# Moving the fourth pair's attention logits ahead of the output projection, with a fourth masked-logit buffer

## The reference, cut to what matters

```python
def block(args):                        # one block of 128 query rows, 8 heads
    ...
    _, sel = lax.top_k(iscore, topk)    # 256 keys chosen per row
    logits = jnp.einsum('bthc,btkc->bthk', ql_b, kv_sel)
    logits = jnp.where(valid[:, :, None, :], logits, -jnp.inf)
    probs = jax.nn.softmax(logits, axis=-1)
    return jnp.einsum('bthk,btkc->bthc', probs, kv_sel)
...
y_dsa = jnp.einsum('bshc,hcd->bshd', o_lat, w_uv[i]).reshape(B, S, DSA_WIDTH)
mix = jnp.concatenate([y_ret, y_dsa], axis=-1) @ w_out[i]
x = x + rms_norm(mix, post_mix_g[i])
f = rms_norm(x, pre_ffn_g[i])
```

## Time and profile before

| | value |
|---|---|
| three executions | 1429.82, 1430.89, 1433.61 us |
| span of the profiled execution | 1428.3 us |
| PE, DVE, ACT, POOL busy | 96%, 71%, 42%, 23% of the span |
| granted TensorE clock, mean | 0.995 |
| attention stage, 456 to 657 us | 201 us, PE busy 181.4 us |

### The profile page before, as it was taken

The page is one execution under the profiler, slowest core; times in us unless marked ns, Lnnn a source line. Parts: engine busy times, 40 slices in busy tenths (PEclk is TensorE's granted clock), DMA queues, the critical chain, the costliest instruction groups (busy, mean ns, idle before and its releaser), DMA issues.

```text
span 1428.3 us, 19391 instructions
## 1 busy us (share of the span) xinstructions
PE 1376.4 (96%) x7142; PEld 1125.8 (79%) x7142; DVE 1013.1 (71%) x1592; ACT 605.1 (42%) x1229; POOL 329.0 (23%) x383
## 2 busy tenths in 40 slices
PE   7999999999989889998999999999999999999998
PEld 7887888887777567777778888888887888888886
DVE  5748789998999546765877777777776765565633
ACT  6434552315823776574522222222222656453221
POOL 4545457711541475652000000000000000000000
PEclk9999999999999999999999999999999999999999
DMA  6322223225323021133234555444458866662211
GB/s 215 82 56 71 79 84 116 94 92 192 111 101 143 31 74 61 45 91 107 55 131 165 177 177 177 161 148 153 156 193 289 316 239 223 237 213 75 67 53 45
DMA packets 137150, 189.02 MB, mean 132 GB/s; under 512 B 12768, under 2 KB 75616, under 8 KB 137056
## 3 DMA queue, kind: packets, MB, share of 16 engines
q1 hardware_dynamic: 120224, 152.17, 32.5%
q10 hardware_dynamic: 16832, 35.61, 6.5%
HBM read 130.08 MB, written 57.67 MB: 131 GB/s over the span
## 4 chain that ended last, share of the span: by engine, by line
PE 79%; DVE 7%; issue 4%; ACT 4%; POOL 3%; DMA 1%; DVEq 1%; SPq 0%; ACTq 0%; POOLq 0%
PE ps L728 23%; PE ps L729 23%; PE ps L730 23%; PE ps L930 2%; PE ps L922 2%; PE ps L941 1%; PE ps L769 1%; POOL mxs L2721 1%; DMA raw<-in_w_in 1%; DVE sc L1915 1%; ACT lm L1444 1%; DVEq L1931 1%; PE ps L857 1%; PE ps L892 1%; PE ps L855 1%
## 5 line engine op out<-in xcount | busy, mean ns | idle before, releaser
L2593 POOL TENSOR_TENSOR smf<-smf,sml 128x1 f32<-128x1 f32 x16 | 9.1, 579 | 739.3 <-DVE smf L2474 625.2
L728 PE MATMUL ps<-bh,ah 128*128 128x512 f32 x308 | 120.1, 390 | 2.4 <-DVE u2b L2315 2.4
L730 PE MATMUL ps<-bh,al 128*128 128x512 f32 x308 | 119.9, 389 | 0.0
L729 PE MATMUL ps<-bl,ah 128*128 128x512 f32 x308 | 119.8, 389 | 0.0
L728 PE MATMUL ps<-wbh,xth 128*128 128x512 f32 (+1 forms) x320 | 118.9, 371 | 0.0
L729 PE MATMUL ps<-wbl,xth 128*128 128x512 f32 (+1 forms) x320 | 117.7, 368 | 0.0
L730 PE MATMUL ps<-wbh,xtl 128*128 128x512 f32 (+1 forms) x320 | 117.7, 368 | 0.0
L2421 DVE TENSOR_TENSOR al<-ra,ah 128x512 fp32r<-128x512 f32 x77 | 53.1, 690 | 70.7 <-ACT ah L1671 70.3
L728 PE MATMUL ps<-th,ssh 128*128 128x512 f32 x240 | 93.6, 390 | 1.8 <-DVE u2b L2291 1.2
L730 PE MATMUL ps<-th,ssl 128*128 128x512 f32 x240 | 93.4, 389 | 0.0
L729 PE MATMUL ps<-tl,ssh 128*128 128x512 f32 x240 | 93.4, 389 | 0.0
(11 more groups left out here) (375 smaller groups left out, 3871.1 us busy)
## 6 DMA issues: line engine op xcount, KB each, us to landing
raw<-in_w_in SPq DMA_DIRECT2D x49, 256.0 KB, 3.0
wt<-in_w_ffn_down SPq DMA_DIRECT2D x44, 256.0 KB, 7.2
down_sums<-wt ACTq DMA_DIRECT2D x44, 256.0 KB, 5.0
ra<-hidden_sums SPq DMA_DIRECT2D x44, 256.0 KB, 2.9
rb<-down_sums SPq DMA_DIRECT2D x44, 256.0 KB, 3.5
raws<-in_w_ffn_gate SPq DMA_DIRECT2D x21, 512.0 KB, 3.9
raws<-in_w_ffn_up SPq DMA_DIRECT2D x21, 512.0 KB, 5.3
ret_rows<-stg SPq DMA_DIRECT2D x32, 320.0 KB, 3.4
```

What stands on the lines that cost most here:

```text
L728: pe.matmul(o, ah, wh, start=start, stop=False, skip_group_check=resumes)
L729: pe.matmul(o, ah, wl, start=False, stop=False, skip_group_check=resumes)
L730: return pe.matmul(o, al, wh, start=False, stop=stop, skip_group_check=resumes)
```

## The change

The pair logits of step t+2 are issued in step t, behind the first part of the probability products and in front of the output projection, at the seven places. DVE masks head t+2 right behind head t+1, in step t+1, ahead of the search pieces and of the probability copy of that step. ACT takes the exponential of head t+1 in step t+1, in front of `read_mix`, instead of in step t+2 behind `mix_square`. A fourth LM tile is added (4 KB per partition at offset 200.5), and LM is used modulo 4, so that `mask_logits(t)` waits for the transposes of head t-4 instead of t-3. Since the new tile overlaps WL[1], `second_gate_lo` waits for the last transposes of LM. Nothing is computed that was not computed before, and no DMA is moved.

```diff
-    LM = [sb(f"lm{i}", [P, S], a) for i, a in enumerate((112, 116, 164))]
+    LM = [sb(f"lm{i}", [P, S], a) for i, a in enumerate((112, 116, 164, 200.5))]
...
+    def before_projection(t):
+
+        return at_block(t, OUT_LAG) is not None and t + 2 < STEPS
...
         for t in range(STEPS + TAIL):
-            if t < STEPS and t % 2 == 0:
+            if t < STEPS and t % 2 == 0 and not before_projection(t - 2):
                 pair_logits(t // 2)
...
+            if before_projection(t):
+                pair_logits(t // 2 + 1)
             if at_block(t, OUT_LAG) is not None:
                 out_projection(at_block(t, OUT_LAG), 0)
...
-            if 1 <= t <= STEPS:
+            if 1 <= t <= STEPS and not before_projection(t - 2):
                 exponent(t - 1)
+            if before_projection(t - 1):
+                exponent(t)
             if at_block(t, OUT_LAG + 1) not in (None, RT - 1):
                 read_mix(at_block(t, OUT_LAG + 1))
...
-            if t >= 3:
-                dve.wait_ge(s["t_tp"], tp_at[("tr", t - 3)] + 1)
+            if t >= len(LM):
+                dve.wait_ge(s["t_tp"], tp_at[("tr", t - len(LM))] + 1)
...
         def second_gate_lo():
             dve.wait_ge(s["a_gh"], 2)
+            dve.wait_ge(s["t_tp"], tp_at[("tr", STEPS - 1)] + 1)
...
-            if t < STEPS:
+            if t < STEPS and not before_projection(t - 2):
                 mask_logits(t)
+            if before_projection(t - 1):
+                mask_logits(t + 1)
```

More of the change, by code:

```diff
@@ L929, in prob_transposes @@
             for j in range(b + 1):
-                m = pe.transpose(pair(2)[:, j * P:(j + 1) * P], LM[t % 3][:, j * P:(j + 1) * P], ID)
+                m = pe.transpose(pair(2)[:, j * P:(j + 1) * P], LM[t % len(LM)][:, j * P:(j + 1) * P], ID)
             m.then_inc(s["t_tp"], 1)
@@ L1443, in exponent @@
             c = (b % 2) * H + h
-            sc.activation(LM[t % 3][:, 0:keys], LM[t % 3][:, 0:keys], ACT.Exp, scale=-1.0,
+            sc.activation(LM[t % len(LM)][:, 0:keys], LM[t % len(LM)][:, 0:keys], ACT.Exp, scale=-1.0,
                           bias=cols["nmax"][:, t % 4:t % 4 + 1], accum_out=cols["sum"][:, c:c + 1])\
@@ L2109, in mask_logits @@
             dve.wait_ge(s["t_lg"], t // 2 + 1)
-            if t >= 3:
-                dve.wait_ge(s["t_tp"], tp_at[("tr", t - 3)] + 1)
-            v.tensor_tensor_reduce(LM[t % 3][:, 0:keys], pair(t % 2, keys), mask, -1.0, 3.0e38, ALU.add, ALU.min,
+            if t >= len(LM):
+                dve.wait_ge(s["t_tp"], tp_at[("tr", t - len(LM))] + 1)
+            v.tensor_tensor_reduce(LM[t % len(LM)][:, 0:keys], pair(t % 2, keys), mask, -1.0, 3.0e38, ALU.add, ALU.min,
                                    cols["nmax"][:, t % 4:t % 4 + 1]).then_inc(s["v_lm"], 1)
```

## The result

The changed kernel took 1438.63 us (median of 4 runs, 1438.36 to 1439.59), the kernel before 1430.94 (4 runs on the same chip, 1429.82 to 1433.61): 1.0054 of before, 95% interval 1.0041 to 1.0067. The forecast was 1438.0 us.

What follows compares the result with a forecast made beforehand. PE, busy 96% of the span, was taken to bound the kernel, with waits at X3 for ACT's chain. 1428.3 + 6.1 (later X3) + 1.1 (DVE beside POOL) = 1435.5, with 2.6 for the median about 1438 us; range 1431.5 to 1442.

Steps and rivals of the forecast that it cites:

- The trade on PE and ACT: Seven places: moved logits and mask waits delay projections 10.8 us in all; exponentials leaving ACT's chain save 5.7 at most.
- the delay minus the exponential: Places 0 to 3, ACT's chain: X3 comes later by 1.04, 0.34, 0.68 and 0.55 us.
- X3's wait at places 0 to 3 smaller in PE idle time: Sign expected in the profile after: PE idles less at X3 there, though X3 comes later in time; no size given.
- Rival A: Seven places: logits cost 7.6, exponentials return 5.7, so 1.9 us slower, 1432.8; chance 0.20 with anything else within 4.3 us.
- rival B: Faster: logits ahead of the projections are free and the exponentials' 5.7 us are gained, 1425.2 us; chance 0.08.
- Place 6: PE's order binds: X2 waits for DVE's copy of X1, X2 and X3 2.3 us later, the exponential's saving worth nothing.
- Place 5: DVE's copy comes behind a search starting about 2.7 us later; X2 1.68 later, X3 0.2 after its 1.48 wait absorbs some.
- 0.24 us at place 5 where the same overlap comes up: Cost of DVE's search overlapping POOL's addition at place 5: 0.24 us, ends 0 and 1.3.
- no wait that an earlier mask or exponential would shorten: PE's queue after X3 goes on as before, so the 6.1 us sum is carried on in full.
- The search beside POOL: POOL's addition waits for DVE's later search piece: 0.83 us at place 3, 0.24 at place 5, 1.1 in all.
- rival C: End of steps: standing before X2 at place 6 lowers PE's clock sooner, two product groups 1.5 us each, 1441; 0.12 with D.
- Rival D: DVE's early mask delays the copy of X1, X2 waits everywhere; up to 1 us each from place 3, 1442; 0.12 with C.

Runs made afterwards that it cites:

- run 1: Kernel before with only the exponential of head t+1 moved in front of read_mix: 1425.2 us, 0.9963 of before; a repeat gave 1425.26 us, 0.9955.
- run 2: Changed kernel with the exponential of head t+1 back in its old place behind mix_square: 1443.11 us, 1.0085 of before.
- run 5: Two kernels against before: logits, mask and exponential moved at places 0 to 3 only, 1433.25 us (1.0015); at place 6 only, 1433.41 us (1.0013).
- run 3: Changed kernel with DVE's mask of head t+2 back behind the search pieces and the copy: 1437.27 us, 1.0032 of before.
- run 7: Changed kernel with 24 extra identity transposes on PE between X1 and X2 at place 5: 1438.68 us, 1.0054 of before.
- run 4: Changed kernel with logits, mask and exponential moved at place 5 only: 1434.49 us, 1.0023 of before.
- run 6: Kernel before with the fourth LM tile and the new wait before WL[1], no place moved: 1431.08 us, 1.0005 of before.

## Why the prediction was right, point by point

**The trade on PE and ACT: right.** The logits stand directly in front of the projection, with waits for DVE's mask of 1.49 at place 0 and 0.88 at place 6 (0.51 of the first is the wait that the projection had there). What follows X3 comes later at places 0 to 4, by 1.24 us over the first two and 0.43 to 0.73 at each other, as the delay minus the exponential said. One sign of the prediction failed at places 0 and 1: X3's idle time grew from 1.18 to 1.39 us, and at place 1 from 0.81 to 1.08, where the prediction had "X3's wait at places 0 to 3 smaller in PE idle time". Runs 1 and 2 show the exponential's side, 0.7 to 0.85 us at each of places 2 to 4, and run 5 the net. Rival A (even) fell with the masks' waits; rival B's 1425.2 is what the exponential gives without the logits (run 1), so its second half, that the logits in front are free, is what is wrong with it. That the number is met is luck in part: the stretches gave 4.9 us for B's 5.7, and the tail 1.5 that B had not counted.

**Place 6: right** (2.33 predicted, 2.30 measured, alone and in the whole). PE's own order, X1, copy, X2, binds there, and the exponential is worth nothing: run 1 too left that stretch at 30.98.

**Place 5: the term that was mis-sized.** The step was "X2 is 1.68 later, X3 0.2" and "0.24 us at place 5 where the same overlap comes up". Measured from the mark in front of the place, X2 came 3.45 us later and X3 4.29 (611.36 before, 619.19 after), and the stretch grew by 3.86. Runs 3 and 7 take it apart. With the masks in the old order the stretch is 29.29, a gain of 0.95 (more than foreseen: the FFN copy behind X3 is waited for 0.60 instead of 1.19 us, which the prediction ruled out with "no wait that an earlier mask or exponential would shorten"). With the masks moved and the clock held it is 31.42, so the lengthened piece costs 2.13, near its own 2.71 - 0.69. Without the filler it is 34.10, so the clock costs 2.68 in this trace (1.35 less in run 2's). -0.95 + 2.13 + 2.68 = 3.86.

**The search beside POOL: a collision foreseen, but priced mostly at the wrong place, and against the wrong engine.** The 0.83 us at place 3 did not come. The rank piece took 1.83 in the earlier trace rows beside POOL; it now runs when POOL is idle, takes 1.09, and is all but over as POOL's addition starts:

```profile
554.63 1.09 DVE L1983 SCALAR_TENSOR_TENSOR rank_c<-rank_c,tie_c 128x896 bf16<-128x896 bf16 x1
```

```profile
555.61 2.36 POOL L2732 TENSOR_TENSOR mxs<-mxa,mxs 128x1024 f32<-128x1024 f32 x1 [3.80 <-ACT mxa L1489]
```

The prediction had kept the duration of a piece that owed it to its neighbour. At place 5 the addition started 0.46 us ahead of the DVE piece (609.61 and 610.07) and ended at 612.23, the piece at 612.78: nearly the piece's own 0.69 behind it. It was DVE that waited, in front of a copy that PE needed. The Trainium skill (SBUF — State Buffer, section "SBUF: two separate sides") says that a DVE instruction in a two-port mode and a GpSimd instruction exclude each other as well: the one that starts first has the shared pair of ports for its whole instruction, and the other blocks. This case's trace agrees, at 2.71 against 0.69 us, though no view shows the mode of L1988. It has one input tile, so it is not of the two-input kind that the prediction named, and the prediction took from the rule only that POOL would wait. No run moved POOL's addition alone: that POOL is the cause rests on the start times, in the traces of after and of runs 2 and 4 (2.71 and 2.72 us inside the addition) against before and run 3 (0.69 outside it).

**The clock: foreseen as rival C, elsewhere.** It fell at place 5, behind the 3.27 us in which PE did nothing, and not at the tail, which came out at full clock (1.97 for 3.51). Worth +2.7 and -1.5. So 1438.0 was near 1438.6 in part by errors of both signs: +3.4 at place 5, -0.83 for the collision at place 3, -0.6 over the other places and terms, -1.5 in the tail, +0.5 ahead of the stage, and -0.6 since the median lies 2.0 us above the profiled span and not 2.6.

**Rival D** (DVE is late with the copy of X1, and X2 waits for it) was true of place 5 alone, by a piece that it did not name. X2 waits for the copy at places 3 and 4 too (0.97 and 1.11 us, within their terms), but there DVE had finished its search and stood for X1 itself, 1.70 us at place 4 and 0.72 at place 3:

```profile
556.44 0.82 DVE L2127 COPY pt<-ps 128x640 f32<-128x640 f32 x1 [0.72 <-PE ps L934]
```

**Open.** Why one execution has the last products at 1.97 and another at 3.51 (run 6, with before's order, had 3.51 again, and run 7 had 3.61), why the low clock at place 5 ended sooner in run 2, and where most executions of run 3 lose 4 us of clock: only one execution of each kernel has a trace.

## What to carry to other kernels

Before an operation is moved ahead of another in one engine's queue, ask which copies behind it another engine waits for, and what runs on POOL at the time at which the operations in between now fall: a duration read beside a busy POOL, or beside an idle one, does not move with the instruction. Test each part of a bundle alone; here the exponential alone gained 0.4%, and the logits and masks moved with it made the whole 0.5% slower. To find a microsecond among runs that scatter by five, measure from one fixed wait to the next in the traces, which here repeated within 0.1 us, and only then the medians.

## What the runs showed of the hardware

- A DVE tensor_scalar over 128x1024 f32 (L1988) took 2.71 and 2.72 us when it started 0.46 us into a POOL addition of 2.6 us, and 0.69 when no such addition was running. The addition itself took 2.62 and 2.63 there, and 2.36 at place 3.
- A PE gap of 3.27 us was followed by a stretch of 6 us at a granted clock of 0.53, the 28 products in it taking 3.26 us for 1.75; behind the same gap in run 2 they took 2.35. With 2.79 us of transposes in that gap the work behind it was at full clock.
- The mean granted clock of whole executions of one kernel ran from 0.991 to 0.997 over the runs of run 1, and their times from 1429.98 to 1423.39 us.
